# Two transformer blocks in one kernel: the norms between stages in two blocks of 256 tokens

## The reference

```python
def modulate(h, shift, scale):
    return h * (1 + scale[:, None, :]) + shift[:, None, :]
# block 1
h = modulate(rms_norm(x, ffn1_norm), sh1, sc1)
x = x + 0.5 * g1 * ((silu(h @ w_gate) * (h @ w_up)) @ w_down)      # FFN1, hidden 2816
h = modulate(rms_norm(x, mix_norm), sh2, sc2)
z = h @ w_in                        # Fourier part, latents of the attention, gate logits
y = (gate_a * fourier(z) + gate_b * mla_attention(z, positions)) @ w_out
x = x + g2 * y
h = modulate(rms_norm(x, ffn2_norm), sh3, sc3)
x = x + 0.5 * g3 * swiglu_2(h)                                     # FFN2
x = rms_norm(x, final_norm)
# block 2
h = rms_norm(x, g_pre_mix) * (1 + sc1) + sh1
o = concat(nsa_attention(h @ w_in), dsa_attention(h @ w_in)) @ w_out
x = x + gt1 * rms_norm(o, g_post_mix)
h = rms_norm(x, g_pre_ffn) * (1 + sc2) + sh2
y = square(relu(h @ w_up)) @ w_down                                # FFN3, hidden 4096
x = x + gt2 * rms_norm(y, g_post_ffn)
```

## Time and profile before

| | us |
|---|---|
| runs (3) | 2074.18, 2074.76, 2074.07 |
| median | 2074.18 |
| the profiled execution's own time | 2074.3 |
| its span in the trace | 2072.5 |
| PE busy | 1936.2 (93%) |
| DVE busy | 1212.3 (58%) |
| POOL busy | 1150.9 (56%) |
| ACT busy | 363.2 (18%) |
| mean granted clock of TensorE | 0.966 |

### The profile page before, as it was taken

The page is one execution under the profiler, slowest core; times in us unless marked ns, Lnnn a source line. Parts: engine busy times, 40 slices in busy tenths (PEclk is TensorE's granted clock), DMA queues, the critical chain, the costliest instruction groups (busy, mean ns, idle before and its releaser), DMA issues.

```text
span 2072.5 us, 25215 instructions
## 1 busy us (share of the span) xinstructions
PE 1936.2 (93%) x8980; PEld 1526.7 (74%) x8980; DVE 1212.3 (58%) x1822; ACT 363.2 (18%) x749; POOL 1150.9 (56%) x1075
## 2 busy tenths in 40 slices
PE   6999999989899999899999978985999979999997
PEld 3788888868657888788888847664666748788785
DVE  7888478746644124887078355675774367405713
ACT  2100000022145111200000031112555230000001
POOL 3577777756440667576777643575000338767861
PEclk8999999999999999999999989896999989999998
DMA  8654555422220234454355221233000112233231
GB/s 277 203 175 158 189 167 183 151 85 89 64 62 1 62 102 140 129 189 132 118 191 172 89 68 41 81 72 93 1 1 1 41 41 87 95 101 94 89 101 40
DMA packets 231130, 216.51 MB, mean 104 GB/s; under 512 B 20305, under 2 KB 227342, under 8 KB 231054
## 3 DMA queue, kind: packets, MB, share of 16 engines
q1 hardware_dynamic: 230000, 214.84, 32.7%
q10 hardware_dynamic: 1054, 0.66, 0.1%
HBM read 213.39 MB, written 2.10 MB: 104 GB/s over the span
## 4 chain that ended last, share of the span: by engine, by line
PE 86%; DVE 10%; ACT 1%; issue 1%; POOL 1%; DMA 0%; ACTq 0%; DVEq 0%; POOLq 0%; SPq 0%
PE ps L614 24%; PE ps L616 24%; PE ps L615 23%; PE ps L891 5%; PE ps L914 4%; PE ps L900 3%; DVE rb L1437 1%; PE ps L660 1%; DVE tt L1931 1%; DVE tt L1654 1%; DVE xT L1932 1%; DVE ada_sum L1466 1%; DVE score L1815 1%; PE ps L645 1%; PE ps L851 0%
## 5 line engine op out<-in xcount | busy, mean ns | idle before, releaser
L525 POOL TENSOR_TENSOR w_lo<-raw,w_hi 128x512 fp32r<-128x512 f32 (+2 forms) x612 | 798.7, 1335 | 12.8
L614 PE MATMUL ps<-h_hi,w_hi 128*128 128x512 f32 x1424 | 565.6, 397 | 28.1 <-DVE h_lo L1459 26.7
L615 PE MATMUL ps<-h_lo,w_hi 128*128 128x512 f32 x1424 | 557.7, 392 | 0.0
L616 PE MATMUL ps<-h_hi,w_lo 128*128 128x512 f32 x1424 | 557.6, 392 | 0.0
L518 POOL TENSOR_TENSOR w_hi<-raw,ones 128x8 fp32r<-128x8 f32 x153 | 34.6, 226 | 870.1 <-PE ps L616 820.5
L614 PEld LDWEIGHTS ps<-h_hi,w_hi 128*128 128x128 f32 x1424 | 269.5, 189 | 92.0 <-issue 35.1
L1466 DVE SCALAR_TENSOR_TENSOR ada_sum<-ada,cT,ada_sum 128x256 f32<-128x256 f32 x378 | 325.1, 860 | 13.4
L615 PEld LDWEIGHTS ps<-h_lo,w_hi 128*128 128x128 f32 x1424 | 269.5, 189 | 58.0 <-issue 2.4
L616 PEld LDWEIGHTS ps<-h_hi,w_lo 128*128 128x128 f32 x1424 | 269.1, 189 | 57.8
L614 PE MATMUL ps<-g_hi,w_hi 128*128 128x512 f32 x608 | 237.4, 390 | 3.1 <-ACT sg L1396 3.1
L616 PE MATMUL ps<-g_hi,w_lo 128*128 128x512 f32 x608 | 236.7, 389 | 0.0
(11 more groups left out here) (274 smaller groups left out, 2239.3 us busy)
## 6 DMA issues: line engine op xcount, KB each, us to landing
ada<-in_ada_w SPq DMA_DIRECT2D x31, 1024.0 KB, 5.3
ada<-in_w_ada SPq DMA_DIRECT2D x24, 1024.0 KB, 6.6
raw<-in_ffn_w_gate SPq DMA_DIRECT2D x22, 1024.0 KB, 6.8
raw<-in_ffn_w_up SPq DMA_DIRECT2D x22, 1024.0 KB, 5.1
raw<-in_w_in SPq DMA_DIRECT2D x16, 1024.0 KB, 5.1
raw<-in_w_up SPq DMA_DIRECT2D x16, 1024.0 KB, 5.2
raw<-in_w_down SPq DMA_DIRECT2D x16, 1024.0 KB, 5.0
raw<-in_ffn_w_down SPq DMA_DIRECT2D x16, 768.0 KB, 4.3
```

The lines of the kernel that those rows point to most:

```text
L525: last = pool.tensor_tensor(lo[:, c], src[:, c], hi[:, c].bitcast(F32), ALU.subtract)
L614: pe.matmul(o, wh, xh, start=start, stop=False)
L615: pe.matmul(o, wh, xl, start=False, stop=False)
L616: return pe.matmul(o, wl, xh, start=False, stop=stop)
```

## The change

Tokens 0 to 255 are called A here, 256 to 511 B.

- `last_pair`: the last two tiles of a stage's output projection (one tile at W_OUT and W_OUT2) are computed for A in PSUM banks 2 and 3, both tiles, and then for B in banks 6 and 7; the norm's sum of A (`half_sum`) stands inside B's products.
- `boundary`, `half_inverse`, `half_scaled`, `half_low` on DVE and `boundary_high` on ACT do the norm for A and then for B; DVE's two additions of B and its reciprocal stand inside A's chunks.
- `first_tiles`: the next stage's tile 0 is computed for A, then for B, then tile 1 for A and B; the sum of B stands after chunk 3 of A. FFN2's and FFN3's first two tiles leave their loops for this.
- The tiles in `EXTRA` are split into a third buffer pair (`we_hi`, `we_lo`), so that POOL's split of them and of the following ones waits for an earlier tile (`n - 3`, `last_user`).
- Norms 3 and 4 become one: PE's sum for norm 4 is taken over squares weighted by `gain2` = final gain squared + eps (a second sum `sq_sum2` on DVE), root with `tiny` = eps squared, factor times the final gain. The final norm's own root (`y_sum`, `y_std`) comes after tile W_IN2+1, and `block1_out`, 8 operations that write it into `xT`, goes among the later projections together with its reciprocal (`block1_root`).
- Block 2's rotations of the index queries and keys go after the second and fourth block of `nat`, and `rotate2` between the copies of `nat`; `nat` waits for `y_std`.
- Norm 6 is summed by PE over eight half squares (`mid_sum`), A before and B after tile 0's A half.
- The mixer's angles are in three parts with branch copies between: two after the first part, two after the second, four after the third.
- In the second half of FFN1 the ada steps stand after the second and third pair of down tiles rather than the second and fourth.
- The end: norm 7 by halves, 16 half chunks of transposes and copies, 8 output transfers of 256 rows x 256 columns.

```diff
+EXTRA = (W_MIX, W_FFN2, W_IN2, W_FFN3)
+    we_hi = place("we_hi", [P, SLOT], F32R, at=at(20))     # we_lo alike
-    DIRECT = (4, 6)
+    SUMMED = (N_FFN1, N_MIX, N_FFN2, N_PRE2, N_POST2, N_POST3)
...
 def split(...)                                             # POOL
-            if not first:
+            if per:
                 pool.wait_ge(tile_used, i * per + (n - 1))
+            elif n in EXTRA:
+                pool.wait_ge(tile_used, n - 3)
+            elif not first:
+                pool.wait_ge(tile_used, last_user(n) + 1)
...
+        def half_sum(i, h):                                # PE
+            pe.matmul(o, ones[:], (sq_sum2 if i == N_PRE2 else sq_sum)[:, t], start=True, stop=False)
+            for m in range(ON_DVE, NC):
+                weight = gain2[:, m:m + 1].broadcast_to([P, P]) if i == N_PRE2 else ones[:]
+                last = pe.matmul(o, weight, sq[:, m % 2, t], start=False, stop=m == NC - 1)
...
+        def last_pair(i, tiles, kc, xh, xl, ready=lambda u: None):
+            for u, n in enumerate(tiles):
+                pe.wait_ge(split_done, n + 1)
+                for m in range(2):
+                    last = part(ps[:, 2 + m, HALF[0]], n, kc, m, xh, xl, kc * u, HALF[0], u == 0, n == tiles[-1])
+            for u, n in enumerate(tiles):
+                for m in range(2):
+                    last = part(ps[:, 6 + m, HALF[1]], n, kc, m, xh, xl, kc * u, HALF[1], u == 0, n == tiles[-1])
+                    if m == 1:
+                        last.then_inc(tile_used, 1)
+                    if u == 0 and m == len(tiles) - 1:
+                        half_sum(i, 0)
+
+        def first_tiles(n0, banks, a0, b0, between, after=lambda: None, first_done=None):
+            for u in range(2):
+                n = n0 + u
+                pe.wait_ge(split_done, n + 1)
+                for h in range(2):
+                    for k in range(NC):
+                        pe.wait_ge((lo_a, h_lo_done)[h], (a0, b0)[h] + k + 1)
+                        for m in range(2):
+                            last = mm3(ps[:, banks[2 * u + m], t], wh[:, k, c], wl[:, k, c], h_hi[:, k, t], h_lo[:, k, t],
+                                       k == 0, k == NC - 1)
+                        if h == 0 and u == 0 and k == 3:
+                            between()
+                    if h == 1:
+                        last.then_inc(tile_used, 1)
...
-        norm_sum(1)
+        first_tiles(W_MIX, (0, 1, 2, 3), 0, 8, lambda: half_sum(N_MIX, 1), first_done=win_mm)
...
+        first_tiles(W_IN2, (1, 0, 4, 7), 16, 24, lambda: half_sum(N_PRE2, 1), first_done=rp_mm)
+        pe.matmul(ps[:, B_NORM], ones[:], sq_sum[:], start=True, stop=False)
+        for m in range(ON_DVE, NC):
+            last = pe.matmul(ps[:, B_NORM], ones[:], sq[:, m % 2], start=False, stop=m == NC - 1)
+        last.then_inc(y_sum, 1)
...
             signal(last, nat_mm, c, NQ, tiles=2)
+            if c % 2:
+                rot(8 + c, R64, P, rp_raw2)
+                rot(9 + c, R64, P, rp_raw2)
...
+        def boundary(i, add, factor, shift, a0, b0):       # DVE
+            for m in range(ON_DVE, NC):
+                add(m, 0)
+                if m == ON_DVE:
+                    norm_add(i, ON_DVE - 1)
+            half_inverse(i, 0)
+            half_scaled(0, 0, factor, a0)
+            add(ON_DVE, 1)
+            for m in range(1, NC + 1):
+                if m < NC:
+                    half_scaled(m, 0, factor, a0)
+                half_low(m - 1, 0, shift, a0)
+                if m == 2:
+                    add(ON_DVE + 1, 1)
+                if m == 6:
+                    half_inverse(i, 1)
             for m in range(NC + 1):
+                if m < NC:
+                    half_scaled(m, 1, factor, b0)
+                if m:
+                    half_low(m - 1, 1, shift, b0)
...
-        angles(0, pos1[:], tab1)
-        for j in range(NC):
+        angles_turns(0, pos1[:])
+        for j in range(2):
+            branch_out(j)
+        angles_rest(0)
+        for j in range(2, 4):
+            branch_out(j)
+        angles_tables(0, tab1)
+        for j in range(4, NC):
+            branch_out(j)
...
-        norm_inverse(3)
-        chunks_then_add(4, final_norm)
-        norm_inverse(4)
-        modulated(3, A_PREMIX, 72)
+        boundary(N_PRE2, lambda m, h: add_half(N_PRE2, m, h, W_IN2 - 1, column(fac, A_G3 + m)), A_PREMIX, 72, 16, 24)
...
+        block1_root()
         for i in range(4):
             rotate2(4 + i, qn[:, i])
+            block1_out(i)
             select(2)
...
+        half_inverse(N_POST2, 0)
+        for m in range(NC):
+            add_normed(m, 0, A_POSTMIX, mid_x)
+            if m in (0, 2):
+                copy_half(ON_DVE + m // 2, 1)
+        half_inverse(N_POST2, 1)
+        for h in range(2):
+            if h:
+                for m in range(NC):
+                    add_normed(m, 1, A_POSTMIX, mid_x)
+            half_inverse(N_PRE3, h)
+            for m in range(NC + 1):
+                if m < NC:
+                    half_scaled(m, h, A_PREFFN, (24, 32)[h])
                 if m:
+                    half_low(m - 1, h, 72 + 24, (24, 32)[h])
```

More of the change, by code:

```diff
@@ L368, in build, with place_of, flat, in_loop @@
         arrived[n] = 16 * loads_before[n % 2]
+    def place_of(n):
+        return (n - sum(e < n for e in EXTRA)) % 2
+    def flat(t, n):
+        if t is raw:
+            return raw[:, n % 2]
+        if n in EXTRA:
+            return (we_hi if t is w_hi else we_lo)[:]
+        return t[:, place_of(n)]
+    def in_loop(n):
+        return n + 2 if n in EXTRA else n
+    def last_user(n):
+        return max(k for k in range(n) if k not in EXTRA and place_of(k) == place_of(n))
     def slot(t, n, kc, cols):
-        return t[:, n % 2, 0:kc * cols].rearrange("p (k c) -> p k c", c=cols)
+        return flat(t, n)[:, 0:kc * cols].rearrange("p (k c) -> p k c", c=cols)
     def ffn_tiles(i):
@@ L538, in _ @@
                     split(1, NC, 256, first=True)
-                with pool.Fori(1 if n0 == 0 else 0, iters) as it:
+                elif n0 == W_FFN2:
+                    for u in range(4):
+                        split(n0 + u, NC, 256)
+                with pool.Fori({0: 1, W_FFN2: 2}.get(n0, 0), iters) as it:
                     for u in range(2):
@@ L546, in _ @@
             n0 = W_FFN3 + 16 * half
-            with pool.Fori(0, 4) as it:
+            if half == 0:
+                for u in range(4):
+                    split(n0 + u, NC, 256)
+            with pool.Fori(2 - 2 * half, 4) as it:
                 for u in range(2):
@@ L639, in norm_sum @@
         def norm_sum(i):
-            if i:
-                pe.wait_ge(n_std, i)
-            if i in DIRECT:
-                for m in range(NC):
-                    pe.wait_ge(n_sq, 8 * i + m + 1)
-                    last = pe.matmul(ps[:, B_NORM], ones[:], sq[:, m % 2], start=m == 0, stop=m == NC - 1)
-                    last.then_inc(n_acc if m < NC - 1 else n_sum, 1)
-                return
             pe.wait_ge(n_acc, last_added(i))
@@ new lines, in mid_sum, with part @@
+        def mid_sum(h):
+            t = HALF[h]
+            for m in range(NC):
+                pe.wait_ge(mid_sq, NC * h + m + 1)
+                last = pe.matmul(ps[:, B_ADA, t], ones[:], sq[:, m % 2, t], start=m == 0, stop=m == NC - 1)
+                last.then_inc(mid_acc if m < NC - 1 else (sum_a, n_sum)[h], 1)
+        def part(o, n, kc, m, xh, xl, k0, t, start, stop):
+            wh, wl = slot(w_hi, n, kc, 256), slot(w_lo, n, kc, 256)
+            c = slice(P * m, P * m + P)
+            for k in range(kc):
+                last = mm3(o, wh[:, k, c], wl[:, k, c], xh[:, k0 + k, t], xl[:, k0 + k, t],
+                           start and k == 0, stop and k == kc - 1)
+            return last
@@ L748, in run_ffn @@
                 pe.wait_ge(mod_read, (4, 5, 7, 7)[2 * i + half])
-                first = i == 0 and half == 0
-                if first:
-                    gate_up(0, 0, 0, tiles=(1,))
-                with pe.Fori(int(first), iters) as it:
+                if half == 0:
+                    if i == 0:
+                        gate_up(0, 0, 0, tiles=(1,))
+                    else:
+                        first_tiles(n0, (0, 1, 2, 3), 8, 16, lambda: half_sum(N_FFN2, 1))
+                        for u in range(2):
+                            ada_mm_step(s0 + u)
+                with pe.Fori(1 - half, iters) as it:
                     gate_up(i, half, it)
@@ L975, in _ @@
                     signal(last, wo_mm, i, 2)
-        for i in range(2, 8):
+        for i in range(2, 6):
             n = W_OUT + i // 2
@@ L1113, in _ @@
         pe.wait_ge(o_lo_done, 12)
-        for i in range(8):
+        for i in range(6):
             n = W_OUT2 + i // 2
@@ L1159, in norm_squares @@
+    def norm_squares(act, i, ready, first, src, chunks=range(NC)):
+        for m in chunks:
             act.wait_ge(ready, first + m + 1)
```

450 lines of the change are left out of this document (311 added, 139 removed).

## The result

| | before | changed |
|---|---|---|
| median (5 runs each) | 2074.76 us | 2093.45 us |
| profiled execution, own time | 2074.3 | 2093.45 |
| its span | 2072.5 | 2091.7 |
| mean granted clock | 0.966 | 0.958 |

The ratio is 1.0081, 95% interval 1.0067 to 1.0096: the changed kernel is 0.8% slower, 14 to 20 us. The kernel before comes at two levels, near 2074.5 and near 2080 us, and the ratios take the mean over runs (2076 to 2078), so a ratio can say up to 4 us more gain than the traces do, in which the kernel before is at its lower level. The first view of the changed kernel is the page's busy line; it answers to the earlier trace rows.

A forecast was written before the change was run, and what follows sets the result against it. PE, busy 93%, was taken to bound the kernel, with DVE in sequence at each boundary. Stages summed to -19.9 us, +2.3 with POOL slowing DVE; plus 5 for the clock, 2074.3 became 2081.6 us, range 2050 to 2093.

The forecast's parts named there:

- The company of POOL: A's chunks at four boundaries: DVE slowed while POOL splits, 2.44 us a chunk rather than 0.92; 22.2 us in all.
- Rival 1: A's chunks at each boundary: DVE is not slowed by POOL and the clock holds; 2054.4 us, chance 0.28.
- A's start R: Time A's reciprocal starts at a boundary; forecast 427.7, 826.8, 1210.1 and 1666.2 us.
- R + 32.6: Each boundary's step sum: tile 1 of the next stage is used 32.6 us after A's reciprocal starts, without POOL's slowing.
- My sum without POOL: All stages without POOL's slowing of DVE: 0.0 - 1.0 - 13.5 + 3.1 + 0.5 - 9.0 = -19.9 us.
- The template: One boundary step by step from A's reciprocal: B's first chunk at 12.9 us, its chunks done 21.1, tile 1 32.6.
- The blocks' boundary: Between the blocks: one norm instead of two in a row; -21.7 us to tile 1 and `nat`, -13.5 after later losses.
- Before FFN3: Boundary before FFN3: four more reciprocals and 32 more small operations fill what was won; +3.1 us, POOL's slowing +4.7 besides.
- The clock: A's chunks at four boundaries: thin PE work lowers the granted clock; 0 to 11 us, taken as +5.
- rival 2: Every boundary: the clock falls, on top of POOL's slowing of DVE; 2087.6 us, chance 0.20.
- The angles: Mixer's angles: copies between parts remove PE's 6.68 us wait and the half-clock products behind it; -9.0 us (0 to -9.5).
- Rival 3: All boundaries: DVE has room for A beside B's products, so PE's idle time closes; 2033.7 us, chance 0.10.

The follow-up runs named there:

- quiet kernel: The changed kernel with POOL's third split at each of the four boundaries held back until B's last h_lo is written; 0.9979 of the kernel before.
- fillers: Quiet kernel plus products of ones by ones where PE waits: 1.0062 with 24, 24, 8 and one per chunk; 0.9987 with 12, 12, 6.
- full-width kernel: The kernel before with norms 3 and 4 as one over all 512 tokens: 0.9991; with the angles in three parts too: 0.9935.

## Why the prediction was right or wrong

**Direction and size.** Slower was the likeliest case, at 2081.6. The median came to 2093.45, half a us past the range's end; by the ratio, on the 2074.3 of the forecast, it is 2091.1, inside it. The forecast took +7.3 and the runs show +16.8 (0.0081 x 2074.76). The sign was right and for its main reason; the size was short by more than half.

**The company of POOL: right in kind, some 4 us too large.** I took 22.2 us (6.3, 4.9, 6.3, 4.7). Against the 7.1 to 7.5 us that these stretches of DVE take without it, A's chunks took 3.8, 3.7, 6.1 and 4.5 more, 18.1 in all; the edit that removes most of it gained 21 by the ratio and 16 at the boundaries. Rival 1, that DVE would not be slowed, is refuted: 1.37 to 1.48 us rather than 0.48. The first boundary was the furthest off, 3.8 against 6.3. The third split there is one of smaller pieces, which I had priced as a whole one, and DVE's operations beside it took 0.7 to 1.1 us:

```profile
437.45 3.94 POOL L570 TENSOR_TENSOR w_lo<-raw,w_hi 128x320 fp32r<-128x320 f32 x4
```

The Trainium skill ("SBUF — State Buffer", section "SBUF: two separate sides") has the loser of the shared ports blocked for the winner's whole instruction. From that I had estimated 1.7 us an operation, where the earlier trace rows gave 1.22. Measured were 1.37 to 1.48 beside pieces of 1.39 (5.54 / 4), about halfway between the two. Three DVE operations in a row started 1.52 and 1.30 apart (831.73, 833.25, 834.55), one for each piece on the mean; that agrees in kind with the rule of one at a time.

**The terms that failed: A's start R, and R + 32.6.** My sum without POOL was -19.9; the quiet kernel has 0.9979, -4.4, and its trace -2.3. This gap of 15.5 us is larger than the whole error of 9.5; the +5 for the clock hid most of the difference, and that is luck. By the quiet kernel's trace, with its lead before each boundary taken off (its own times of R: 431.04, 824.13, 1212.34, 1659.89):

| | FFN1 to mix | mix to FFN2 | blocks | before FFN3 |
|---|---|---|---|---|
| R later than forecast | 2.1 | 1.2 | 4.7 | 1.3 |
| from R to tile 1 used | 35.8 | 33.6 | 36.0 | 55.9 |
| forecast for it | 33.1 | 32.6 | 32.6 | 54.5 |

```profile
1212.34 1.75 DVE L1661 RECIPROCAL rb<-std 128x256 f32<-128x256 f32 x1 [5.80 <-ACT std L1331]
...
1224.54 1.75 DVE L1661 RECIPROCAL rb<-std 128x256 f32<-128x256 f32 x1 [1.65 <-ACT std L1331]
```

So some 9 us lie in A's start and 8.5 behind it. The template said that "PE's A products (5.8) and the sum of B (1.45) lie beside DVE's A chunks". PE does them beside, but B's sum stands behind chunk 3 of A, and B's reciprocal waited for it at each of the first three boundaries, 1.9, 1.6 and 2.5 us in the changed kernel, 1.5, 1.0 and 1.7 in the quiet one. That wait stands in no term. Since B's reciprocal comes before the end of A's chunks, it still started at R + 12.0, 9.9 and 12.2 (forecast 11.2), and those of the first and third hold the 1.7 us of company that was left. The end of A's chunks follows it instead, and from B's reciprocal to tile 1's end it is 23.7 or 23.8 us at all three, not 21.4. The run with the table load out of the way shows at the first boundary that an earlier A doesn't start B earlier; the sum one chunk earlier points the same way. The chunk at 0.92 and the reciprocal at 1.75 were exact.

**A's start R.** At the first boundary it was 430.8 rather than 427.7. The parts: 1.0 from the start of the program, the waits of 1.2 for the ada step ahead of A's first products, half clock after it (PEclk 0.57 from 416 to 420, the window below; I estimate 1.7 us, 4.00 x 0.43), and 1.28 for the table load, which in the kernel before ran under the sum. None was in my sum. What was in it, a stall of 2.8 for the last down tile, didn't come: PE was late enough. That leaves 0.7 us that I can't place.

```profile
416.00:420.00 4.00, 4.00 (x23) 4.00 (x22) 3.41 (x7) 0.63 (x1) 4.00 (x6) 0.57 0.27 92
```

**The blocks' boundary.** -21.7 was -13.6 without company. R was 1212.3 in the quiet kernel, which came to this boundary 2.5 us early, so 4.7 later than my 1210.1. PE stood 3.22 us for the last down tile, near the 2.8 that I took from the first boundary, and then ran at half clock (PEclk 0.57 from 1198 to 1206 in the quiet kernel), which I had not; with fillers A's start came 2.5 us earlier. In the changed kernel this wait is the row

```profile
1207.12 0.39 PE L665 MATMUL ps<-g_hi,w_hi 128*128 128x256 f32 x1 [3.22 <-POOL w_lo L570]
```

The +6.7 to the scores was near (5.2 to 5.9, of a stage in which the kernel with the angles alone is 2.4 late). The final norm's work on DVE I had at +1.5, bounds 0 and 8.7; leaving it out of the full-width kernel gave 6.

**Before FFN3.** +3.1 was +5.7. PE sums norm 6 from two buffers of squares, so that ACT and PE take turns: 0.87 us per chunk. I had that sum hidden under `add_normed`. DVE in the changed kernel:

```profile
1694.53 1.75 DVE L1659 RECIPROCAL rb<-std 128x256 f32<-128x256 f32 x1 [4.28 <-ACT std L1329]
```

4.28 us of waiting for it, none of which stands in my sum.

**The clock.** I had +5, between 0 and 11, as a term beside the company. In the changed kernel the clock fell to half at all four boundaries (rival 2 was right in that), but DVE's rows leave about 1 us of the 16 at the boundaries for it to have cost by way of the company. With POOL quiet it fell at three, and there the fillers gave under half a us inside A's chunks and some 2 us ahead of A's start between the blocks, a place that my term did not have in view.

**The angles** were right, -9.0 against -9.8. **The tail** was right within what a stage can be read to.

**Rival 3** needed DVE to have room for A; the waits for `h_lo` rose.

**The split products** took 0.12 each as in the earlier trace rows. What stays open is what full clock would give in the changed kernel with POOL at work, and which part of the rest of the change makes it slower than the full-width kernel with the same fused norms and angles; neither was tried.

## What to carry to other kernels

Halving the tokens of a norm starts the next stage earlier only if the slowest engine of the norm is free while the first half is in work; here a helper that had been given one buffer more ran beside it and made its operations up to three times as long, which cost more than all else in the change gave. In a chain of halves, look for what the second half waits for (here its sum, queued behind the first half's products), since an earlier start of the first can be lost there. Holding a helper back moves its work to another place: look what runs there. And work that is moved into an engine's slack is hidden only up to the next stretch that this engine sets.

## What the runs showed of the hardware

- DVE operations with two SBUF inputs, 128x256, took 0.48 us alone and up to 1.53 beside a GpSimd subtraction with two inputs (1.29 to 1.39 a piece); additions with one input from PSUM (0.47) and reciprocals (1.75) were the same in both.
- Before FFN2 PE waited 4.35 us, and the granted clock was then 0.53 over six us, at 0.50 (the 1.2 GHz level) in most of it; where PE waited 2.62 at the same place, it stayed at 1.00. At the first boundary of the quiet kernel it was 0.50 after a wait of 3.57.
- ACT's table load stood behind the last wait written ahead of its activation: at 429.02 with PE's sum last, at 424.85 with the waits swapped. It delays the activation by its 1.28 us where that wait is the late one.
- A plain float32 product of 128 columns took two passes of 0.115 us: 24 of them show as 48 and took 5.52.
